# Block sums of a Strassen-Winograd product: from a DRAM scratch to VectorE adds on loaded blocks

## The reference

```python
def conv_ffn(h, p):                               # first block: h is 1024 x 1024
    u = dwconv(h @ p['w_up'], p['ffn_conv']) + p['ffn_conv_b']
    val, gate = jnp.split(u, 2, axis=-1)
    return (val * jax.nn.silu(gate)) @ p['w_down']
...
h2 = rmsnorm_2(h_res, g_ffn_pre[l])               # second block: 1040 rows, the halves swapped
up = centred_dwconv(h2 @ w_up[l], conv_w_ffn[l], conv_b_ffn[l])
a, v = jnp.split(up, 2, axis=-1)
ffn_out = (jax.nn.gelu(a) * v) @ w_down[l]
```

## Time and profile before

| | |
|---|---|
| median of 3 runs | 3827.13 us (3824.38 to 3827.26) |
| the profiled execution, its own time | 3828.93 us |
| its span in the trace | 3827.1 us |
| TensorE busy | 89% of the span |
| VectorE busy | 59% |
| ScalarE busy | 41% |
| mean granted TensorE clock | 0.938 of full |

### The profile page before, as it was taken

How to read it: one execution, slowest core, us unless ns; L and a number is a source line. 1 busy time by engine, 2 the same in 40 slices (tenths; PEclk the granted TensorE clock), 3 DMA queues, 4 the chain that set the end, 5 groups by cost and what they waited for, 6 DMA issues and landing times.

```text
span 3827.1 us, 72929 instructions
## 1 busy us (share of the span) xinstructions
PE 3424.5 (89%) x30711; PEld 3114.0 (81%) x30711; DVE 2276.1 (59%) x3617; ACT 1580.3 (41%) x2735; POOL 234.1 (6%) x399
## 2 busy tenths in 40 slices
PE   8999978867798989889999996499999999999999
PEld 4787778867787778667788996379999989999999
DVE  5477756756575764776776883122223577777576
ACT  4566633333234764533344552111113443334454
POOL 2000000000000000000000112100000000000110
PEclk9999989888898999999999998699999999999999
DMA  6244455457523305333345766961113333344675
GB/s 234 74 143 136 142 201 185 162 126 175 136 64 77 80 29 145 97 108 110 114 136 186 264 214 232 253 133 38 45 50 91 117 103 111 108 140 122 240 243 163
DMA packets 396766, 528.85 MB, mean 138 GB/s; under 512 B 20596, under 2 KB 311895, under 8 KB 392345
## 3 DMA queue, kind: packets, MB, share of 16 engines
q1 hardware_dynamic: 353160, 332.72, 28.5%
q0 software_dynamic: 43280, 191.47, 17.2%
HBM read 441.17 MB, written 175.21 MB: 161 GB/s over the span
## 4 chain that ended last, share of the span: by engine, by line
PE 45%; DVE 6%; issue 3%; DMA 3%; ACT 2%; another core or an unknown queue 2%; DVEq 2%; ACTq 0%; POOL 0%
PE psum L3587 8%; PE psum L3588 7%; PE psum L3589 7%; PE psum L2849 4%; PE psum L2850 4%; PE psum L2851 4%; PE psum L2370 3%; PE psum L2372 3%; PE psum L2371 3%; DMA down_w_raw<-in_w_down 1%; DMA down_w_raw<-in_w_in 1%; DVE mix_u_val L3877 1%; DVE mix_u_gate L3877 1%; PE psum L3488 1%
## 5 line engine op out<-in xcount | busy, mean ns | idle before, releaser
L2236 DVE TENSOR_TENSOR down_w_lo<-down_w_raw,down_w_hi 128x1024 fp32r<-128x1024 f32 x228 | 270.5, 1187 | 562.2 <-ACT down_w_hi L2210 559.9
L2210 ACT ACTIVATE down_w_hi<-down_w_raw 128x1024 fp32r<-128x1024 f32 x228 | 234.7, 1029 | 695.5 <-PE psum L2851 283.5
L3434 DVE TENSOR_TENSOR mix_w_split<-mix_w_raw,mix_w_split 128x512 fp32r<-128x512 f32 x372 | 255.4, 688 | 296.1 <-ACT mix_w_split L3430 295.8
L2370 PE MATMUL psum<-down_ghi,down_w_hi 128*128 128x256 f32 x1408 | 404.1, 287 | 11.7 <-DVE down_glo L2241 11.5
L2372 PE MATMUL psum<-down_glo,down_w_hi 128*128 128x256 f32 x1408 | 399.5, 284 | 0.0
L2371 PE MATMUL psum<-down_ghi,down_w_lo 128*128 128x256 f32 x1408 | 399.2, 284 | 0.0
L3587 PE MATMUL psum<-mix_t_hi,mix_w_split 128*128 128x258 f32 (+1 forms) x1056 | 339.9, 322 | 13.7 <-DVE mix_t_lo L3815 13.6
L3588 PE MATMUL psum<-mix_t_hi,mix_w_split 128*128 128x258 f32 (+1 forms) x1056 | 339.3, 321 | 0.0
L3589 PE MATMUL psum<-mix_t_lo,mix_w_split 128*128 128x258 f32 (+1 forms) x1056 | 339.0, 321 | 0.0
L2849 PE MATMUL psum<-h_hi,down_w_hi 128*128 128x348 f32 (+2 forms) x768 | 254.1, 331 | 74.1 <-DVE down_w_lo L2236 35.8
L3430 ACT ACTIVATE mix_w_split<-mix_w_raw 128x512 fp32r<-128x512 f32 x372 | 228.0, 624 | 155.7 <-PE psum L3589 134.4
(11 more groups left out here) (499 smaller groups left out, 8537.1 us busy)
## 6 DMA issues: line engine op xcount, KB each, us to landing
down_w_raw<-in_w_down SPq DMA_DIRECT2D x176, 512.0 KB, 4.3
up_sums<-in_w_up POOLq DMA_DIRECT2D x48, 1408.0 KB, 20.1
mix_w_raw<-up_sums SPq DMA_DIRECT2D x176, 256.0 KB, 2.9
mix_w_raw<-in_w_up SPq DMA_DIRECT2D x132, 256.0 KB, 3.1
up_sums<-up_sums POOLq DMA_DIRECT2D x16, 1408.0 KB, 24.6
g_scratch<-mix_u_val POOLq DMA_DIRECT2D x44, 512.0 KB, 3.6
down_w_raw<-in_w_in SPq DMA_DIRECT2D x36, 512.0 KB, 4.0
down_g_part<-g_scratch POOLq DMA_DIRECT2D x6, 2816.0 KB, 16.6
```

The source lines that it names most:

```text
L2210: self.nc.scalar.activation(self.hi[s][:, 0:w], self.raw[s][:, 0:w], ACT.Copy).then_inc(self.w_high, 1)
L2236: last = self.nc.vector.tensor_tensor(self.lo[s][:, 0:w], self.raw[s][:, 0:w], self.hi[s][:, 0:w].bitcast(F32), ALU.subtract)
L2370: nc.tensor.matmul(out, w_hi[:, w], g_hi[:, :], start=(n == 0 and c % 2 == 0), stop=False, skip_group_check=True)
L3434: nc.vector.tensor_tensor(ring[s % 4][:, 1, :], raw[s % RAWS][:, :], ring[s % 4][:, 0, :].bitcast(F32), ALU.subtract).then_inc(w_low.sem, 1)
```

## The change

Four things are changed.

1. **No sums in DRAM.** `sum_weights`, its 64 DMAs, the tensors `up_sums` and the waits for them are gone.
2. **VectorE makes the sums.** For each pair five tiles are loaded, in the order A11, S1, S3, A12, A22; S1 and S3 are both A21. Before P6 VectorE waits for four of them and makes three adds, 128 x 512 each (`first_sum`): S1 += A22 (for P5), S3 += A11 (for P7), and after a drain A11 += S1 (for P6). A fourth add, A12 += A11 (for P3), comes after the low part of P5's weights for an early pair, of P2's for another. `weight_high` of P6, P7, P5 and P3 waits for these adds instead of a load. The ten buffers now hold two pairs.
3. **P3 of an early pair is a step later** where the next pair is not an early one: the P1 of the next pair goes ahead of it. There are seven such places in each mixer.
4. **Shorter chains.** Both token halves follow one schedule: residuals at e = 2 to 5, the second mean at e = 7, the scaling at 9 and 10. That is one step earlier than the second half had it, and four than the first. The first parts of the next products are rounded at 10 and 11 for the first half, and at 14 and 15 for the second.

```diff
@@ second mixer's and first mixer's calls
                 pool.dma_start(k.mod_w[i % 3][:, :], w_mod[:, kk, c:c + MOD_COLS]).then_inc(mod_landed[i % 3], 16)
-                sum_weights(pool, k, 0, i)
...
-        for i in range(32):
-            sum_weights(pool, self.k, 1, i)
@@ plan_steps
+    for at in range(len(late) - 1):
+        if late[at][0] == "P3" and late[at][1] in EARLY and late[at + 1][0] == "P1":
+            late[at:at + 2] = late[at + 1], late[at]
@@ mixer_out_to_ffn
+    tiles += [(what, i, "late") for i in range(KF) for what in ("A11", "S1", "S3", "A12", "A22")]
+    SOURCE = {"P1": "A11", "P6": "A11", "P7": "S3", "P5": "S1", "P2": "A12", "P3": "A12", "P4": "A22"}
...
     def weight_high(act, s):
-        act.wait_ge(*w_landed[s % RAWS].at(landed_at(s)))
+        if kind in ("P6", "P7", "P5"):
+            act.wait_ge(*w_added.at(2 * i + 1))
+        elif kind == "P3":
+            act.wait_ge(*w_added.at(2 * i + 2))
+        else:
+            wait_landed(act, t)
...
     def weight_low(dve, s):
...
+        if s + 1 < STEPS and steps[s + 1][0] == "P6":
+            first_sum(dve, steps[s + 1][1])
+        elif kind == ("P5" if i in EARLY else "P2") and s >= first_late:
+            dve.drain()
+            a11, a12 = (raw[tile_of[what, i, "late"] % RAWS] for what in ("A11", "A12"))
+            wait_landed(dve, tile_of["A12", i, "late"])
+            nc.vector.tensor_tensor(a12[:, :], a12[:, :], a11[:, :], ALU.add).then_inc(w_added.sem, 1)
+
+    def first_sum(dve, i):
+        held = [tile_of[what, i, "late"] for what in ("A11", "S1", "S3", "A22")]
+        for t in held:
+            wait_landed(dve, t)
+        dve.drain()
+        a11, s1, s3, a22 = (raw[t % RAWS] for t in held)
+        nc.vector.tensor_tensor(s1[:, :], s1[:, :], a22[:, :], ALU.add)
+        nc.vector.tensor_tensor(s3[:, :], s3[:, :], a11[:, :], ALU.add)
+        dve.drain()
+        nc.vector.tensor_tensor(a11[:, :], a11[:, :], s1[:, :], ALU.add).then_inc(w_added.sem, 1)
...
     def sync(sp):
-            if s == first_late:
-                for done in k.sums_done:
-                    sp.wait_ge(done, 128 + 128 * spec["mixer"])
@@ VectorE's chain (ScalarE's and TensorE's are moved in the same way)
-                if 3 <= e <= 6:
-                    residual(a, 2 * e - 6, 2 * e - 5)
-                elif e == 8:
+            elif 2 <= e <= 5:
+                residual(a, 2 * e - 4, 2 * e - 3)
+            elif e == 7:
                     means(a, 1)
-                elif e in (10, 11):
-                    scale_rows(a, 4 * e - 40)
+            elif e in (9, 10):
+                scale_rows(a, 4 * e - 36)
```

More of the change, by code:

```diff
@@ L3253 @@
     pass
[L3256 to L3273, removed]
 class Counted:
@@ L3410, in mixer_out_to_ffn, with source, block, tile @@
     up.first_took = max(u[1] for u in upper if u[0] == "took")
-    up.raw_free = [max(s + 1 for s in range(STEPS) if s % RAWS // 2 == j) for j in range(2)]
     after.up = up
-    def source(s):
-        kind, i = steps[s][0:2]
[L3416 to L3422, removed]
-    def weight_high(act, s):
-        act.wait_ge(*w_landed[s % RAWS].at(landed_at(s)))
+    def source(t):
+        what, i = tiles[t][0:2]
+        if what == "O":
+            h = tiles[t][2]
+            return w_out[:, 4 * h:4 * h + 4, i % KD * P:i % KD * P + P]
+        return block(what, i)
+    def block(what, i):
+        low, c = {"A11": (0, 1), "P1": (0, 1), "A12": (4, 1), "P2": (4, 1), "A22": (4, 0), "S1": (0, 0), "S3": (0, 0)}[what]
+        c = (i + side[c]) * P
+        return w_up[:, low:low + 4, c:c + P]
+    def tile(s):
+        kind, i = steps[s][0:2]
+        return s if s < first_late else tile_of[SOURCE[kind], i, "late"]
+    def wait_released(eng, t):
+        what, i = tiles[t][0:2]
+        if t < first_late:
+            eng.wait_ge(*w_low.at(t + 1))
+        elif what == "A11":
+            eng.wait_ge(*w_added.at(2 * i + 2))
+        else:
+            eng.wait_ge(*w_low.at(index[{"S1": "P5", "S3": "P7", "A12": "P3", "A22": "P4"}[what], i] + 1))
+    def wait_raw(eng, j):
+        for slot in (2 * j, 2 * j + 1):
+            wait_released(eng, max(range(slot, TILES, RAWS)))
+    def wait_landed(eng, t):
+        eng.wait_ge(*w_landed[t % RAWS].at(landed_at(t)))
+    up.wait_raw = wait_raw
+    def weight_high(act, s):
+        kind, i = steps[s][0:2]
+        t = tile(s)
+        if kind in ("P6", "P7", "P5"):
+            act.wait_ge(*w_added.at(2 * i + 1))
+        elif kind == "P3":
+            act.wait_ge(*w_added.at(2 * i + 2))
+        else:
+            wait_landed(act, t)
         if s >= 4:
@@ L3435, in weight_low @@
                                 ALU.subtract).then_inc(w_low.sem, 1)
-    def sync(sp):
-        for s in range(STEPS):
-            if s >= RAWS:
-                sp.wait_ge(*w_low.at(s - RAWS + 1))
-            elif before and s < 4:
-                sp.wait_ge(before.low, before.total - 1 + s // 2)
+        if s + 1 < STEPS and steps[s + 1][0] == "P6":
[5 more added lines that the diff above has]
+            nc.vector.tensor_tensor(a12[:, :], a12[:, :], a11[:, :], ALU.add).then_inc(w_added.sem, 1)
@@ L4076, in second_mixer @@
         active_first=True, left=META - first - 1, dst=0, pads=(2 * n,), before=down1, after=down2,
-        follows=mix1, mixer=1, slot_order=(0, 3, 2, 1)))
+        follows=mix1, slot_order=(0, 3, 2, 1)))
     return mix2
```

117 lines of the change are left out of this document (45 added, 72 removed).

## The result

The changed kernel takes **3695.86 us** (median of 4 runs, 3694.18 to 3700.93) where the kernel before takes 3827.2; the ratio is 0.9658, with a 95% interval of 0.9641 to 0.9675. Forecast were 3722 us, within 3660 to 3782. The profiled execution took 3696.23 us, its span is 3694.4 us, and the mean granted clock rose from 0.938 to 0.965. So the span is 132.7 us shorter; forecast were 105.

What follows compares the result with a forecast made beforehand. Bounds: late loads beside the sums in scan and second block; in mixers TensorE and P3's wait. Profiled 3828.9 - 94 - 5 - 95 + 85 + 4 = 3723.9 us, so median 3722 us, range 3660 to 3782.

Steps and rivals of the forecast that it cites:

- Sums out of the scan, and the first loads: Scan: unit loads no longer late beside the sums, 15 units -94 us (bounds -60, -170); first loads before it -5.
- Rival D: Scan: loads stay late because of `mod_w` alone, the scan gains nothing, 3821 us; chance 0.03.
- Rival A: Scan: it gives back all its waits, -170 in place of -99, 3651 us; chance 0.14.
- Sums out of the second block: Second block, 2350 to 2540.7 us: `w_in` loads no longer late, 190.7 us become 95, so -95 (bounds -80, -101).
- The rule of turns: DMA queues taking turns packet by packet: a load beside one busy GpSimd queue takes about twice its time alone.
- Adds on VectorE: Mixers: VectorE sets the pace, seven-step pair 22.4 us, double 42.7; +85 in all (bounds +55, +150).
- Rival B: Mixers: ScalarE's rounding waits on the adds, one more handshake of 1.5 us per pair, +65, 3787 us; chance 0.13.
- P3 a step later: Mixers: costs nothing by itself; its worth is in the doubles, where P3's stall goes.
- The loss is P3 waiting for the take of P5: Mixer doubles before the change: time lost to P3's wait, 14 times for 44.8 us, and the lower clock after it.
- Shorter chains: Residual chains before the mixers' products: `mix_h` wait goes, `mix_t_lo` wait stays, together +4 us (bounds -12, +15).
- Rival C: Mixers: TensorE, not fed in time, stays at the low clock; at 0.65 +217, 3939 us; chance 0.06.

Runs made afterwards that it cites:

- experiment 1: Changed kernel with all 64 transfers of the block sums put back on GpSimd's queue, their results unused: 3921.24 us, ratio 1.0219.
- Experiment 2: Changed kernel with the same 64 transfers put back, all as plain copies, none accumulating: 3845.26 us, ratio 1.0046.
- experiment 3: Changed kernel without the four adds of a pair and the waits on them, so another product is computed: 3556.41 us, ratio 0.9275.
- experiment 4: Changed kernel with P3 of an early pair put back before the next pair's P1: 3683.06 us, ratio 0.9599.
- experiment 8: The kernel of experiment 7 with P3 of an early pair put back before the next pair's P1: 3590.38 us, ratio 0.9361.
- Experiment 10: Kernel before the change, with ScalarE's rounding of step s + 4 ahead of the centring of step s: 3777.78 us, ratio 0.9864.
- experiment 7: Changed kernel with ScalarE's rounding of step s + 4 ahead of the centring of step s (P4 and P3): 3583.61 us, ratio 0.9344.
- experiment 9: Kernel of experiment 7, rounding also ahead of P1 and P2 evictions, every P3 behind the next pair's P1, `first_sum` a step earlier: 3566.35 us, ratio 0.9294.

## Why the prediction was right, and where it was off

The four misses don't cancel by much: 22 us more gain than forecast up to the end of the scan, 15 more in the second block, 10 more loss in the mixers, and next to nothing in the chains. That the time falls well inside the range is not luck; that it is 26 us below the point is mostly the two terms for the loads.

*Sums out of the scan, and the first loads: right in mechanism, -121.5 for -99.* The cause is shown by experiment 1: the same transfers bring the 15 units back to 503. Rival D (late because of `mod_w`) is out, with 7.8 us of waiting left. The term was undersized at the units that follow a finishing one: I took 33 us for them from the one row of 34.7 without sums. They took 27.5 and 29.7, 9 us less in all. That row stands for itself: the same unit takes 34.4 us after as well, so the sums were not what held it. The ten ordinary units took 25.3 on average (forecast 26), 7 us less in all, finishing ones 29.5 (29). The first loads gave 12 where I had put 5 without a row for it; the scan's mark lies between 546.1 and 555.4 us in the eight profiles, which makes it 5 to 14. Rival A (-170 for the scan) is out: ordinary units still take 23.8 to 27.5 us with hardly a wait for a load left in them.

*Sums out of the second block: -110 for -95, and outside my bound of -101.* Two sizes were off. The spacing of 0.174 us was taken from the stretch behind, whose mix of matmuls differs, with 5.5 us on top for late loads; there were none, and the stretch took 85.9 us, not 95. And my window ended at 2540.7, while the cost went on: 41.3 us at clock 0.92 became 37.4. The bound of -101 stood on the 89.5 us of that spacing and on that window, and fails with both: 104.8 us were gained inside it and 3.9 behind it. The reading that the 97.0 us busy at clock 0.74 are more than the work was right.

*The rule of turns.* I had taken turns as equal, so "about twice", and let the measurement decide. Experiment 2's rows show nearly one packet for one, but of very unequal length; with that the rule gives the size of what was measured.

*Adds on VectorE: right, +95 for +85.* Pair and double came out at 22.5 and 43.0 for 22.4 and 42.7, and experiment 3 gave back 36.7 for the 36.1 of VectorE without adds. The +95 is a net figure: from experiment 3 to the changed kernel, where only the adds differ, it is +123 (751.4 and 874.4 us for products 0 to 20 of both mixers), and the rest of the change gave 28 back. The wait behind `first_sum` is 0.70 us for the 0.75 of the estimate. What was too small are pairs 0 and 1 (+4.8 and +4.4 for +2 each, of which 1.8 each is the mark of product 1, a step later by the new order) and the doubles of mixer 2 (43.3). Rival B, one more handshake per pair, is out by the same rows.

*P3 a step later: the reason I gave is refuted for the changed kernel.* I wrote that its worth is in the doubles and that P3's stall would go. P3 waits for the take of P5 30 times and for 74.8 us after the change. The step in between gives the take 2.8 us more, but with the take standing in a VectorE loop that is 9 us a double longer than TensorE's work, the slack gathers at whatever TensorE asks for next. With the bound at VectorE (experiment 4) and with it nearly gone (experiment 8) the order is worth nothing that can be measured. Without the adds it is likely worth what I thought: experiment 3 has the new order and 751.4 us where the kernel before has 779.1, P3's waits are 15.8 us for 44.8, and ScalarE waits for no load of weights in the doubles of either. The transfers don't matter there (experiment 1 leaves the mixers as they are after). It isn't shown, since the order of the loads changed with it and no run has the new place of P3 alone.

*"The loss is P3 waiting for the take of P5": true as a row, not as a cause.* Experiment 10 shows that the take was late because of the order on ScalarE that makes the two waits of 1.83 us, which I had read, called latency rather than slack, and then left as given. The same order carried a bit over half of the price of the adds. Products 0 to 20 of both mixers together, in us, the first two rows with P3 in its old place:

| | without adds in the kernel | with adds in the kernel | difference |
|---|---|---|---|
| centring first | 779.1 (before) | 869.2 (experiment 4) | +90 |
| rounding first | 725.8 (experiment 10) | 768.3 (experiment 8) | +42 |
| centring first, P3 later | 751.4 (experiment 3) | 874.4 (after) | +123 |
| rounding first, P3 later | not run | 768.1 (experiment 7) | |
| the order of experiment 9 | not run | 746.5 | |

*Shorter chains: -1 in mixer 1, none that can be told in mixer 2, for +4.* The wait for `mix_h` went as forecast. The one for `mix_t_lo` I expected to stay; it fell from 7.3 to 3.5 us.

*Rival C, the clock, did not come.* The doubles' clock is 0.95 in both mixers, that of the seven-step pairs 1.00, far from the 0.71 from which it would have decided, though TensorE now waits in every pair. In mixer 1 that is 0.94 before and 0.95 after; in mixer 2 it fell from 0.98 to 0.95. The Trainium skill (TensorE: Matmul & The Clock Gate, Why this matters for your kernels) warns of idle gaps between bursts of matmuls. The rows of mixer 1's doubles fit a mild form of it: TensorE's longest wait there was 3.5 us before (clock 0.94), 2.7 after (0.95), 2.0 in experiment 7 (0.96) and 1.1 in experiments 3 and 10 (1.00).

Still open: whether unequal turns of the two queues are why copies cost a load 2.7 times its time. No other queue and no other size of packet was tried.

## What to carry to other kernels

When traffic that nobody is waiting for makes waits elsewhere, moving its arithmetic to an engine can pay even if that engine then sets the pace: here it gained 230 us of waits for loads for 95 us in the mixers. But before paying such a price, look at what that engine's loop already waits for. A wait of an engine that has work left behind it is part of its length, and the order of two instructions on its partner may halve the price: here the rounding ahead of the centring, worth 114 us after and 53 before. A step put in so that one engine needn't wait for another helps only where the other engine isn't the bound. And cut windows by the work that they hold, not by where the idle time seems to end.

## What the runs showed of the hardware

- An accumulating DMA from DRAM to DRAM is slower than a copy of the same bytes: 16.7 us for 10.5 us to land in the scan, and 214 for some 340 GB/s in the second block with the DMA engines equally busy. The profile page's count of bytes read from memory is 426.49 MB with and without accumulation, so that count doesn't show the second operand.
- Loads of 512 KB on SyncE's queue land in 4.8 us beside `mod_w` loads only, in 13.0 beside copies of 1408 KB on GpSimd's queue that come one by one, and in 39.9 and 53.6 us when 32 such calls (plain, or partly accumulating) are queued at once. There the two queues move nearly equal numbers of packets (3875 and 3977 in 100 us), 0.5 KB each for the loads and 8.0 KB each for the copies.
- The same code of the scan took from 392.2 to 406.1 us in eight profiles, far more than the mixers, whose products 0 to 20 took 874.4 to 875.1 us in four profiles of the same code. Differences of 10 us between kernels are better read in the stretch that was edited than in the total.
